# Compress and compressed-score matmuls issued between the blocks of projection units 6 to 9 of the NSA layer

## The reference, cut to what matters

```python
q, kc, vc, ks, vs, kw, vw, gates = jnp.split(h @ w_in, splits, axis=-1)   # ten blocks of 256 columns, and 48 gates
def compress(a, pe, w1, b1, w2):              # 15 overlapping blocks of 32 tokens, 4 groups
    flat = (a[:, :, blk_idx] + pe).reshape(B, G, nc, CMP_BLOCK * dh)       # 60 rows of 2048
    return jax.nn.gelu(flat @ w1 + b1) @ w2   # w1 is 2048 x 256, w2 is 256 x 64
k_cmp = compress(kc, cmp_pe[0], cmp_w1[0], cmp_b1[0], cmp_w2[0])
v_cmp = compress(vc, cmp_pe[1], cmp_w1[1], cmp_b1[1], cmp_w2[1])
logits_c = einsum('bgrsd,bgcd->bgrsc', q, k_cmp) * scale + bias_c          # 16 heads x 256 x 15
p_c = masked_softmax(logits_c, mask_c);  o_cmp = einsum(p_c, v_cmp)
o = g[0] * o_cmp + g[1] * o_sel + g[2] * o_win;  return o @ w_out
```

## Time and profile before

| what | value |
|---|---|
| three runs | 1121.44, 1127.84, 1128.02 us |
| median | 1127.84 us |
| profiled execution, first to last instruction | 1123.3 us |
| profiled execution, mean granted TensorE clock | 0.982 |
| PE busy | 1096.9 us (98%) |
| PEld busy | 1002.0 us (89%) |
| DVE, ACT, POOL busy | 574.9, 482.6, 104.9 us |

### The profile page before, as it was taken

One profiled execution on the slowest core, in us unless ns is written; L12 is line 12 of the kernel. 1 busy time (PEld: TensorE's weight loads), 2 busy tenths in 40 slices (PEclk: granted clock), 3 DMA queues, 4 the chain that ended last, 5 costly groups with the idle time before them and its releaser, 6 DMA issues.

```text
span 1123.3 us, 18174 instructions
## 1 busy us (share of the span) xinstructions
PE 1096.9 (98%) x7545; PEld 1002.0 (89%) x7545; DVE 574.9 (51%) x645; ACT 482.6 (43%) x613; POOL 104.9 (9%) x206
## 2 busy tenths in 40 slices
PE   7999999999999999999999999999999999999997
PEld 6888999899966679999998999999899779999996
DVE  4544445652266555544446544544645666544544
ACT  5434343452244335343444434334554835334332
POOL 0100000211023220000002000000206410000000
PEclk9999999997969999999999999999999999999999
DMA  8785655476300137556555665565465235565551
GB/s 276 232 287 195 190 184 186 149 228 205 113 1 1 38 93 245 178 175 205 172 176 168 198 198 176 186 192 182 153 196 177 76 113 177 181 200 176 183 187 38
DMA packets 137814, 187.79 MB, mean 167 GB/s; under 512 B 7249, under 2 KB 120102, under 8 KB 137766
## 3 DMA queue, kind: packets, MB, share of 16 engines
q1 hardware_dynamic: 133702, 172.86, 47.8%
q0 software_dynamic: 3920, 14.18, 3.8%
q10 hardware_dynamic: 144, 0.07, 0.0%
HBM read 184.45 MB, written 1.07 MB: 165 GB/s over the span
## 4 chain that ended last, share of the span: by engine, by line
PE 90%; DVE 3%; ACT 2%; issue 1%; POOL 1%; SPq 1%; DMA 1%; DVEq 0%; ACTq 0%
PE ps L927 87%; PE ps L1162 2%; POOL ms_half L338 1%; DVE normed L669 1%; DVE normed L649 1%; ACT ps L459 1%; DMA raw<-in_ffn_w_gate 1%; ACT whi L439 1%; POOL rstd L344 0%; PE ps L1007 0%; DVE xlo L677 0%; DVE res L658 0%; SPq L277 0%; SPq L286 0%; SPq L285 0%
## 5 line engine op out<-in xcount | busy, mean ns | idle before, releaser
L637 DVE TENSOR_TENSOR wlo<-raw,whi 128x2048 fp32r<-128x2048 f32 x156 | 358.2, 2296 | 329.7 <-ACT whi L439 329.5
L927 PE MATMUL ps<-xhi,whi 128*128 128x256 f32 x1536 | 436.6, 284 | 0.0
L927 PE MATMUL ps<-xlo,whi 128*128 128x256 f32 x1536 | 435.5, 284 | 0.0
L927 PE MATMUL ps<-xhi,wlo 128*128 128x256 f32 x1536 | 435.4, 283 | 0.0
L439 ACT ACTIVATE whi<-raw 128x2048 fp32r<-128x2048 f32 x156 | 297.7, 1908 | 112.5 <-PE ps L927 110.6
L927 PEld LDWEIGHTS ps<-xhi,whi 128*128 128x128 f32 x1536 | 295.6, 192 | 2.6 <-issue 1.2
L927 PEld LDWEIGHTS ps<-xlo,whi 128*128 128x128 f32 x1536 | 295.6, 192 | 1.6 <-issue 0.2
L927 PEld LDWEIGHTS ps<-xhi,wlo 128*128 128x128 f32 x1536 | 295.5, 192 | 0.0
L927 PE MATMUL ps<-whi,hhi 128*128 128x512 f32 x320 | 125.0, 391 | 0.0
L927 PE MATMUL ps<-wlo,hhi 128*128 128x512 f32 x320 | 125.0, 391 | 0.0
L927 PE MATMUL ps<-whi,hlo 128*128 128x512 f32 x320 | 124.5, 389 | 0.0
(11 more groups left out here) (167 smaller groups left out, 887.8 us busy)
## 6 DMA issues: line engine op xcount, KB each, us to landing
raw<-in_ffn_w_gate SPq DMA_DIRECT2D x44, 1024.0 KB, 5.4
raw<-in_ffn_w_up SPq DMA_DIRECT2D x44, 1024.0 KB, 5.4
raw<-in_ffn_w_down SPq DMA_DIRECT2D x44, 1024.0 KB, 4.9
raw<-in_fox_w_in SPq DMA_DIRECT2D x12, 1024.0 KB, 5.5
raw<-in_nsa_w_in SPq DMA_DIRECT2D x10, 1024.0 KB, 5.2
big<-in_nsa_cmp_w POOLq DMA_DIRECT2D x2, 2048.0 KB, 9.9
raw<-in_nsa_w_out SPq DMA_DIRECT2D x4, 1024.0 KB, 5.1
raw<-in_fox_w_out SPq DMA_DIRECT2D x4, 1024.0 KB, 4.9
```

Source lines behind the costliest of these rows:

```text
L637: nc.vector.tensor_tensor(wlo[:, slot, :], raw[:, slot, :], whi[:, slot, :].bitcast(F32), ALU.subtract).then_inc(w_lo, 1)
L927: return nc.tensor.matmul(out_, l, r, start=start, stop=stop)
```

## The change

`features` gets a callback `woven`, called ahead of each of the 16 blocks of three matmuls. `compress_hidden(0)` is issued through it inside unit 6, two matmuls (four instructions) ahead of each block; `compress_out(0)` in the middle of unit 7; `compress_hidden(1)` inside unit 8; and 12 of the 16 compressed-score matmuls inside unit 9, the remaining 4 where all stood. ACT's GELUs move behind the evacuation of units 6 and 8, ahead of the `hi` that stood there, and DVE's `gather(1)` moves ahead of the copy of `kcmp`.

```diff
@@ ScalarE
                     for k in range(1, nproj):
                         evacuate(k - 1)
-                        hi_static(u0 + k + 2)
-                        if kind == "nsa" and k == 3:
...
-                        if kind == "nsa" and k in (6, 9):
-                            kv = (k - 6) // 3
+                        if kind == "nsa" and k in (7, 9):
+                            kv = (k - 7) // 2
                             act.wait_ge(hid_mm, kv + 1)
...
                             last.then_inc(hid_ready, 1)
+                        hi_static(u0 + k + 2)
@@ VectorE
                             if k == 7:
+                                gather(1)
                                 dve.wait_ge(cmp_mm, 1)
...
-                            if k == 7:
-                                gather(1)
@@ TensorE
                     for k in range(KT):
+                        if woven:
+                            woven(KT * a + k)
                         last = split_mm(ps[:, bank, a * S:(a + 1) * S], (wh[:, k, a * P:(a + 1) * P], wl[:, k, a * P:(a + 1) * P]),
...
+                def step(i):
+                    if i == 0:
+                        pe.wait_ge(flat_ready, kv + 1)
+                        pe.wait_ge(w1_in[kv], 16)
+                        if kv:
+                            pe.wait_ge(hid_ready, 1)
+                            pe.wait_ge(cmp_ready, 1)
+                    m = i // 8
+                    for k in (2 * (i % 8), 2 * (i % 8) + 1):
+                        last = mm(ps[:, MB, m * 64:m * 64 + G * NC], w1[:, k, m * P:(m + 1) * P], flatv[:, k, :], k == 0, k == 15)
+                    if i == 15:
+                        last.then_inc(hid_mm, 1)
+                return step
...
+            def early_compressed_scores(i):
+                if i == 4:
+                    pe.wait_ge(proj_ready, PROJ0["nsa"] + 9)
+                    pe.wait_ge(gate_ready, 2)
                     pe.wait_ge(cmp_ready, 1)
...
+                if i >= 4:
+                    compressed_score((i - 4) % 2, (i - 4) // 2)
...
+                            woven = {6: compress_hidden(0), 7: lambda i: compress_out(0) if i == 8 else None,
+                                     8: compress_hidden(1), 9: early_compressed_scores}.get(k)
...
-                    if kind == "nsa" and k in (5, 8):
-                        compress_hidden((k - 5) // 3)
-                    if kind == "nsa" and k in (6, 9):
-                        compress_out((k - 6) // 3)
+                    if kind == "nsa" and k == 9:
+                        compress_out(1)
...
-                        for t in range(TT):
-                            for pair in range(H // 2):
...
+                        for pair in range(6, H // 2):
+                            for t in range(TT):
+                                last = compressed_score(t, pair)
```

More of the change, by code:

```diff
@@ L590, in _ @@
                         evacuate(k - 1)
-                        hi_static(u0 + k + 2)
-                        if kind == "nsa" and k == 3:
-                            act.wait_ge(gates_mm, 1)
-                            nc.scalar.activation(gate_e, ps[0:48, OB, 0:S], ACT.Exp, scale=-1.0).then_inc(gate_exp, 1)
-                        if kind == "nsa" and k in (6, 9):
-                            kv = (k - 6) // 3
+                        if kind == "nsa" and k in (7, 9):
+                            kv = (k - 7) // 2
                             act.wait_ge(hid_mm, kv + 1)
@@ L603, in _ @@
                             last.then_inc(hid_ready, 1)
+                        hi_static(u0 + k + 2)
+                        if kind == "nsa" and k == 3:
+                            act.wait_ge(gates_mm, 1)
+                            nc.scalar.activation(gate_e, ps[0:48, OB, 0:S], ACT.Exp, scale=-1.0).then_inc(gate_exp, 1)
                         if kind == "fox" and k == 3:
@@ L940, in wrows, with features @@
                 return [w[:, slot, :].rearrange("p (k n) -> p k n", k=2) for w in (whi, wlo)]
-            def features(u, slot, bank, between=None):
+            def features(u, slot, bank, between=None, woven=None):
                 pe.wait_ge(w_lo, u + 1)
@@ L1095, in compress_hidden, with compressed_score @@
             def compress_hidden(kv):
[L1096 to L1099, removed]
+                def step(i):
[11 more added lines that the diff above has]
+                return step
+            def compressed_score(t, pair):
+                c0 = (t * H + 2 * pair) * NC
+                return mm(ps[:, OB, c0:c0 + 2 * NC], qT[:, pair, t * P:(t + 1) * P], kcmp[:, 2 * pair // G, :, :], True, True)
+            def early_compressed_scores(i):
+                if i == 4:
+                    pe.wait_ge(proj_ready, PROJ0["nsa"] + 9)
+                    pe.wait_ge(gate_ready, 2)
                     pe.wait_ge(cmp_ready, 1)
[L1101 to L1104, removed]
+                if i >= 4:
+                    compressed_score((i - 4) % 2, (i - 4) // 2)
             def compress_out(kv):
@@ L1214, in _ @@
                         by_token = kind == "fox" and k < 4
-                        (tokens if by_token else features)(u0 + k, (u0 + k) % RING, GB + k % 2)
+                        woven = None
+                        if kind == "nsa":
+                            woven = {6: compress_hidden(0), 7: lambda i: compress_out(0) if i == 8 else None,
+                                     8: compress_hidden(1), 9: early_compressed_scores}.get(k)
+                        if by_token:
+                            tokens(u0 + k, (u0 + k) % RING, GB + k % 2)
+                        else:
+                            features(u0 + k, (u0 + k) % RING, GB + k % 2, None, woven)
                     if kind == "nsa" and k == 2:
@@ L1239, in compressed_scores @@
                         pe.wait_ge(cmp_ready, 1)
-                        for t in range(TT):
-                            for pair in range(H // 2):
-                                c0 = (t * H + 2 * pair) * NC
-                                last = mm(ps[:, OB, c0:c0 + 2 * NC], qT[:, pair, t * P:(t + 1) * P], kcmp[:, 2 * pair // G, :, :], True, True)
+                        for pair in range(6, H // 2):
+                            for t in range(TT):
+                                last = compressed_score(t, pair)
                         last.then_inc(sc_mm, 1)
```

## The result

The change is 1.1% slower: 1135.73 us, median of 4 runs (1132.48 to 1136.72), against 1125.47 us for the kernel before (median of 4). The ratio is 1.0109, 95% interval 1.0075 to 1.0143. The forecast was 1125 us, 2.7 us less than the kernel before; measured are 10.3 us more. The time lies outside the forecast's range and near the case called "slower" (1134.4 us).

A forecast was written before the change was run, and what follows sets the result against it. PE was taken to bound the kernel, ending the chain for 90% of the span. From 1127.84 us, -6.4 + 4.0 - 1.0 - 0.5 + 1.2 = -2.7 gave 1125 us, range 1117.5 to 1129.

The forecast's parts named there:

- slower: Case, chance 0.08: the wait at unit 8 drops the clock and the mixed unit does not restore it; +6.6 us, 1134.4 us.
- what the new 4.0 us gap does to the clock: Clock term for PE's new idle ahead of unit 8: bounds nothing, 2.0 or 10.5 us; taken at +1.2 us.
- the low half: Part of the bounds kept for the clock's fall at unit 8: 0 to 2.5 us, taken at +1.2.
- 331 us: Time in the old trace when the clock returned in attention rounds; used as evidence that mixed work restores it.
- Unit 6 mixed: Unit 6 with the first compression inside: no clock fall expected, 12.9 us, from 257.1 to 270.0.
- Idle 4.0: PE waits ahead of unit 8 for the second `w1`, from 276.2 to 280.2: +4.0 us, paid in full.
- The idle behind head 1's scores: Start of the attention: PE idles 2.1 us, not 0.73, until head 0's logits; the clock likelier falls again.
- The start of the attention at full clock: Case, chance 0.25: the attention keeps full clock, 15.9 us and not 22.9, a gain of 7.0; total 1118.6 us.
- The -6.4: Saving from mixing the first compression into unit 6: 4.46 us in the compression and 1.98 in unit 6.
- the first half-clock stretch: PE at half clock from some 2.5 us into the first compression into unit 6; costs 6.4 us, expected to go.
- 1127.84: Median in us taken as base for the kernel before: profile span 1123.3 with 4.5 us around it.
- 0.60: Chance of the forecast case: first half-clock stretch goes, `w1` wait comes, attention starts at half clock; 1125, range 1123 to 1128.

## Why the prediction was wrong, step by step

**The step that failed** is the one on "what the new 4.0 us gap does to the clock". It was bounded from 0 to 10.5 us, and I took +1.2, in "the low half", because the clock had come back at 331 us "in rounds of scores, transposes and values", which I called "thinner work than a mixed unit". The fall cost 10.7 us: the upper end. The trace had two cases of recovery, pure projection work within 4.3 us and the rounds, and one of none, the 9.0 us of 60-column matmuls. I ranked the mixed unit by how much work it seemed to hold. The row of the rounds did not even speak for the low half: before the clock came back at 331 it had been at half for 21.7 us of them, nearly as long as a whole mixed unit takes at half clock. The runs show the order: pure work restored the clock in about 3.5 us, the mixed unit not in 21 to 24 us of half clock, in three traces of three (the change twice, and the run without the second transfer). In all three it came back 1.2 to 3.7 us into unit 9, which begins with pure work. What in the mixture prevents it, the runs do not show.

**The other steps, by their own numbers.** Unit 6 mixed: 12.9 predicted, 12.66 measured, at 1.00. Transfer issued at 270.2 and landed at 280.2: 270.14 and 279.62. DVE's `kcmp` at 279.3: 278.92. Idle 4.0: 3.55. The idle behind head 1's scores 2.1: 2.1, and the clock fell at its start, so that the attention ran at half clock as forecast. Small matmuls between large ones at 0.11 to 0.12 us each: 12.66 us for 112, so 0.113. The compressed scores were to end at 305.8; they ended at 316.7, late by 10.9: the failed term, 10.7. The start of the attention at full clock, 7 us less in 15.9 us: with the idle filled the same stretch took 16.1 us (301.93 to 318.02), and the kernel 1111.0 against 1118.7, 7.7 us less.

**The long idle gap and the transfer.** The page "TensorE: Matmul & The Clock Gate" of the Trainium skill, section "Why this matters for your kernels", was right about the fall behind a long idle gap. The trace agrees: half clock from 280.7, behind an idle of 3.55 us. By it I had named 2.0 to 2.5 us, the price of a recovery in pure work; the mixed unit paid 10.7. The fit that the Trainium skill gives in "SBUF — State Buffer", section on the DMA setup-cost knee, made an estimated 6.8 us for the transfer; it took 9.5 us from issue to landing, and the measurement decides. Without any transfer three of four executions were as slow, so neither number mattered much.

**The -6.4 was counted against the wrong base.** It was read off an execution that had the first half-clock stretch, and in that execution it very nearly came true: PE was ready for unit 8 at 276.4 and not at 282.6. But I took off the sum from 1127.84, and that execution took 1125.1. The stretch is also not in every execution, as the trace with the first compression as a block shows; in how many of the kernel before, I did not trace. Over its 31 executions of the first set, 9 lay near 1117 us and only 3 near 1128. Against their median of 1121.61 the same repair (first compression in unit 6, the rest as a block) is worth 2.9 us. The three runs had seemed to speak for 6.4 us, by a difference of 6.4 to 6.6 between them; beside 31 executions spread from 1116.6 to 1128.3 that agreement carries no weight.

**What the change cost, added up.** Between the two profiled executions: -6.2 up to unit 8, +3.55 of idle, +10.6 for unit 8 with the compression (23.4 against 12.8), -0.6 up to the end of the compressed scores and +0.2 behind them make 7.5, all of the 7.4 measured. Between the medians it is 10.3. The execution profiled first is the fastest of the change; in the second trace the half clock at the attention lasts 27 us and not 20.5, and costs 3.8 us more. From 1121.6 the sum with the measured terms is 1121.6 - 2.9 + 3.55 + 10.7 = 1133, against 1135.7 measured; that the 3 us left are this stretch is a reading of the two traces and not shown for the medians. What sets its length no run shows.

**The chances.** The slower case had 0.08 and named mechanism, place and price. Its argument for (9 us of small matmuls at half clock did not restore it) and against (331 us) were one row each, and I had no ground for 0.60 against 0.08 between them.

## What to carry to other kernels

Before matmuls are moved to an earlier place, list every input of the first one moved and count from the event that releases it; here four waits moved forward by one unit of 6 us, and a chain of ACT and DVE and a 2 MB transfer both lost their cover. Price a new idle on PE (2.6 and 3.5 us here) by what stands behind it: if that is pure dense work, it is the idle and some 2 us; if it is mixed work, count the whole unit at half clock. Where idle time at such a place can't be taken out, fill it with work or with matmuls that nobody reads: 14 of them, 1.7 us, cut this kernel's spread from 14 to 4 us. And before a saving is read off one profile, look whether other executions have the loss at all.

## What the runs showed of the hardware that was not expected

- Idle ahead of unit 8 and what followed: 0.8 us ahead of mixed work, no fall in the profiled execution; 2.6 us, a fall in 3 of 4 executions; 3.5 us, in all 8 of the change, by their times (two of them traced).
- At the start of the attention the clock fell 0.1 to 1.6 us into an idle of 2.1 us in five traces, at the end of idles of 0.3 and 0.8 us or just behind them in two, and with PE busy, ahead of any idle there, in three. With 0.3 and 0.8 us of idle, 5 of 10 executions lost time to it. The half clock then lasted 13 to 38 us in these ten traces.
- The times of the kernel before gather near 1117, 1121.5, 1125 and 1128 us, with a mean clock from 0.986 to 0.979. That the groups differ by where and how long the clock was at half fits the traces; of this kernel only one execution was traced.
- Mixed work keeps a clock of 1.00 (12.7 us in units 6 and 8) and does not restore it (22.7 us at 0.50 in the change, 21 to 24 us in three traces). The same instructions, at two levels.
- A plain float32 matmul with 60 moving columns took 0.112 us per instruction, one of a projection with 256 columns 0.12, and the mixture of both 0.113. All load 128 weight columns; next to no time is saved by the narrower operand.
